# Two layers on one core: a merging step ahead of two modulation chunks, an output tile split by its last block, a pair product between two chunks

## The reference, cut to what matters

```
mod = silu(c) @ w_ada + b_ada                       # shifts, scales, gates
z, xbc, dt, sc_b, sc_c, sc_h, gate_a, gate_b = split(h @ w_in)
y   = gated_rmsnorm(ssd_chunked(silu(conv(xbc)), ...), z)      # 8 groups, 4 chunks of 128 tokens
y_a = y @ w_ssd_out
y_b = (sc_b * conv(sc_c * sc_h)) @ w_sc_out
merged = sigmoid(gate_a) * y_a + sigmoid(gate_b) * y_b
mix = merged @ w_o
x   = layer_norm(ALPHA * x + g1 * mix) * ln1_g + ln1_b
h   = layer_norm(x) * (1 + sc2) + sh2
scores = sigmoid(h @ router_w); top-k routing; 64 experts; shared expert
```

## Time and profile before

| | |
|---|---|
| median of 3 executions | 3117.07 us (3110.25 to 3120.41) |
| profiled execution, own time | 3117.96 us |
| its span | 3116.3 us |
| PE busy | 3010.0 us, 97% |
| DVE busy | 1901.8 us, 61% |
| mean granted clock of TensorE | 0.987 of full speed |

### The profile page before, as it was taken

The page is one execution under the profiler, slowest core; times in us unless marked ns, Lnnn a source line. Parts: engine busy times, 40 slices in busy tenths (PEclk is TensorE's granted clock), DMA queues, the critical chain, the costliest instruction groups (busy, mean ns, idle before and its releaser), DMA issues. The chain is left out here.

```text
span 3116.3 us, 41002 instructions
## 1 busy us (share of the span) xinstructions
PE 3010.0 (97%) x13039; PEld 1842.5 (59%) x13040; DVE 1901.8 (61%) x4044; ACT 583.8 (19%) x1348; POOL 245.6 (8%) x377
## 2 busy tenths in 40 slices
PE   7999999999999999999997998999999999999998
PEld 5767888755548333333332445488744788588543
DVE  5768888577657444334334377665657655665667
ACT  1002333211011122222221216310000233200000
POOL 1000000011100222222213000000000000000000
PEclk8999999999999999999999999999999999999999
DMA  7673232488733599999988321132254324022342
GB/s 258 181 217 124 67 108 87 137 288 288 254 147 146 209 382 382 378 384 370 395 342 285 115 87 56 34 102 81 108 188 156 102 80 142 30 101 81 149 175 108
DMA packets 260030, 570.90 MB, mean 183 GB/s; under 512 B 26969, under 2 KB 154564, under 8 KB 234170
## 3 DMA queue, kind: packets, MB, share of 16 engines
q1 hardware_dynamic: 202896, 415.82, 37.4%
q0 software_dynamic: 46992, 140.43, 12.9%
q10 hardware_dynamic: 10010, 12.92, 1.2%
HBM read 556.32 MB, written 38.93 MB: 191 GB/s over the span
## 5 line engine op out<-in xcount | busy, mean ns | idle before, releaser
L1709 PE MATMUL ps<-WR,hT 128*64 x832 | 373.5, 602 | 23.2 <-issue 21.7
L1710 PE MATMUL ps<-WR,hT 128*64 128x512 f32 x832 | 373.5, 602 | 0.0
L2154 PE MATMUL ps<-WR 128*128 128x512 f32 x784 | 337.4, 592 | 1.0 <-DVEq L3935 0.7
L1709 PEld LDWEIGHTS ps<-WR,hT 128*64 128x64 f32 x832 | 115.2, 139 | 265.0 <-issue 265.0
L2154 PEld LDWEIGHTS ps<-WR 128*128 128x128 f32 x784 | 148.6, 190 | 188.9 <-issue 186.1
L3647 DVE COPY WR<-WR 128x1024 f32 x208 | 130.9, 692 | 161.4 <-SPq L842 106.8
L2113 PE MATMUL ps<-WR 128*128 128x256 f32 x960 | 217.0, 379 | 0.0
L2113 PEld LDWEIGHTS ps<-WR 128*128 128x128 f32 x960 | 182.4, 190 | 24.8
L1730 PE MATMUL ps<-WR 128*64 x416 | 191.2, 603 | 2.8 <-DVEq L3660 1.8
L1731 PE MATMUL ps<-WR 128*64 128x512 f32 x416 | 191.3, 603 | 0.0
L3981 DVE TENSOR_TENSOR WR<-ps,WR 128x256 f32<-128x256 f32 x210 | 86.1, 423 | 145.0 <-PE ps L2113 143.2
(11 more groups left out here) (533 smaller groups left out, 5054.1 us busy)
## 6 DMA issues: line engine op xcount, KB each, us to landing
WR<-in_w_gate SPq DMA_DIRECT2D x64, 1024.0 KB, 8.5
WR<-in_w_up SPq DMA_DIRECT2D x64, 1024.0 KB, 10.9
WR<-in_w_down SPq DMA_DIRECT2D x64, 1024.0 KB, 10.2
WR<-in_mlp_w SPq DMA_DIRECT2D x56, 1024.0 KB, 6.8
WR<-in_mlp_w SPq DMA_DIRECT2D x20, 2048.0 KB, 8.2
xr<-in_ada_w POOLq DMA_DIRECT2D x32, 1024.0 KB, 5.6
WR<-in_w_in SPq DMA_DIRECT2D x24, 1024.0 KB, 7.5
WR<-in_w_in SPq DMA_DIRECT2D x40, 512.0 KB, 8.0
```

The lines of the kernel that those rows point to most:

```text
L1709: mm(out[0:HALF], xT[u][:, k, 0:HALF], wa[:, :, k, :], start=(k == 0), stop=(k == KD - 1))
L1710: last = mm(out[HALF:P], xT[u][:, k, HALF:P], wb[:, :, k, :], start=(k == 0), stop=(k == KD - 1))
L2154: return mm(ps[:, bank, :], rows, weights, start=(row == 0), stop=(row == PAST[phase] - 1))
```

## The change

It has three parts. First, in the last calls of turn 0 on PE the part 1 of the pair is cut in two: p7 goes between chunk 0 and chunk 1, and p3 and p4 stay behind chunk 1. In the other turns the order stays what it was. Second, the first output tile waits for seven merging steps instead of eight, takes the sum over partitions and blocks 0 to 6 of both halves, then waits for the eighth step and takes block 7 of both halves. Third, on DVE `merged(1)` goes ahead of the last two of six chunks of its step.

```diff
@@ ssd_pair on PE
-                else:
+                elif part == 1:
                     pe.wait_ge(*pair_sum(q, "s3"))
                     pe.wait_ge(*pair_c(q, "u2"))
                     product(r1, s3, t3, False)
+                else:
                     pe.wait_ge(*pair_sum(q, "s4"))
                     pe.wait_ge(*pair_c(q, "c5"))
                     product(r3, s4, hT_block(1, 1), False)
@@ ssd_turn on PE
                 if c == 0:
                     ssd_pair(p, 1, 0)
                     ssd_chunk(0, c)
+                    ssd_pair(p, 1, 1)
+                    ssd_chunk(1, c)
                 else:
                     ssd_pair(p, 0, 0)
                     ssd_pair(p, 0, 1)
+                    ssd_pair(p, 0, 2)
                     ssd_z_spent(c - 1)
                     ssd_chunk(0, c)
                     ssd_pair(p, 1, 0)
-                ssd_chunk(1, c)
-                ssd_pair(p, 1, 1)
+                    ssd_chunk(1, c)
+                    ssd_pair(p, 1, 1)
+                ssd_pair(p, 1, 2)
                 ssd_chunk(2, c)
@@ PE, after the merging
-            pe.wait_ge(sem("merge_free"), 2 + MERGES)
+            pe.wait_ge(sem("merge_free"), 2 + MERGES - 1)
             ada_sums(0, (MERGES - 1) * ADA_N + ADA_MERGE["sum"], SUM_BANKS[2])
             have("w_o", 0)
             have("w_o", 1)
-            out_tile("w_o", mergedT, 0, 0, 16)
+            for n in range(0, KD - 1):
+                out_tile("w_o", mergedT, 0, n, n + 1)
+            for n in range(KD, 2 * KD - 1):
+                out_tile("w_o", mergedT, 0, n, n + 1)
+            pe.wait_ge(sem("merge_free"), 2 + MERGES)
+            for n in (KD - 1, 2 * KD - 1):
+                out_tile("w_o", mergedT, 0, n, n + 1)
@@ DVE, merging
             gate_sums(0, 1)
-            weigh_part(1, 0, ADA_N)
+            weigh_part(1, 0, 4)
             merged(1)
+            weigh_part(1, 4, ADA_N)
```

## The result

The changed kernel takes 3123.01 us (median of 20 runs, 3113.24 to 3129.16), the kernel before 3116.5 us (20 runs, 3109.2 to 3124.62). The ratio is 1.0017, with a 95% interval of 1.0009 to 1.0025: slower by 3 to 8 us. I had forecast 3114.8 us, 2.3 us less, in a range up to 3121. By the bound of 0.3% this is still no change, but it moved the other way and lies outside the range.

What follows compares the result with a forecast made beforehand. PE, busy 97% of the span, was taken to bound the kernel through its order and waits. 0.5 + 2.8 + 0.2 - 1.2 = 2.3 us less, from 3117.07 to 3114.8 us; range 3108 to 3121.

Steps and rivals of the forecast that it cites:

- Part 1, 0.5 us: Turn 0: p7 covers PE's 1.06 us wait before chunk 1; z projection 0.5 us earlier, bounds 0 and 1.06.
- Part 2, 2.8 us (1.7 to 3.8): First merging iteration: merged(1) ahead of chunks 4 and 5 brings PE's second pair 2.8 us earlier, bounds 1.7 to 3.8.
- 1.0 us of stall: Merging: DVE's assumed wait for the load POOL issues after chunk 4, the middle of 0 to 2.1 us.
- The 4.2 us of PE: Merging: PE alone could reach the second pair at 688.3 instead of 692.43, by idle time and half clock removed.
- Part 3, direct gain 0.2 us: First output tile: ACT finds the first turned tile earlier while DVE waits for `grow`; 0.2 us gained, bounds 0 and 0.5.
- the 3.4 us that PE was to be early: First output tile: PE saves 1.75 us of idle time and 1.7 us of half clock, up to 3.4 us.
- Part 3, the clock, 1.2 us (0 to 2.1): Last `turn_in` and router: longer PE idle time brings half clock behind it, costing 1.2 us, bounds 0 to 2.1.
- I had 3.5: Ahead of the last `turn_in`: PE's idle time forecast at 3.5 us, from 4.2 less some spent earlier.
- The rival "slower": Router: clock stays at half throughout after longer idle time, adding 7.3 us, giving 3120.9 us; chance 0.05.
- `grow` moved with the merging: Rival at the first residual: `grow` lands no earlier, so the merging gain is lost; 3118.3 or 3117.1 us; chance 0.15.
- merged(1) never waited for PE: Rival in the merging: merged(1) comes before the PE product it needs, forecast as 2.8 us ahead; chance 0.02.

Runs made afterwards that it cites:

- e2: The kernel before with the split first output tile alone; 1.0021 (1.0012 to 1.0030) of the kernel before.
- e3: The kernel before with the second product pair of the shared expert's second tile moved behind the router, leaving PE idle; 1.0034 (1.0023 to 1.0044).
- e5: The kernel before with the moved merging step alone, merged(1) ahead of chunks 4 and 5; 1.0001 (0.9989 to 1.0012).
- e1: The changed kernel without the split first output tile; 0.9995 (0.9986 to 1.0005) of the kernel before.
- e6: The changed kernel without the split tile, with merged(1) behind chunk 4 instead of ahead of it; 0.9991 (0.9980 to 1.0002) of the kernel before.
- e9: The changed kernel without the split tile, DVE making corners and next sums after two chunks instead of three in the first merging iteration; 0.9993 (0.9981 to 1.0005).
- e11: e9 with two idle matmuls ahead of the last turned tile and four ahead of the routing counts; 0.9990 (0.9980 to 1.0001) of the kernel before.
- e10: The changed kernel with twelve idle matmuls, results unused, ahead of the last turned tile; 0.9995 (0.9984 to 1.0006) of the kernel before.
- e4: The changed kernel with a quarter of the shared expert's third tile brought ahead of the last turned tile; 1.0000 (0.9989 to 1.0012) of the kernel before.
- e7: The changed kernel with half of the shared expert's third tile brought ahead of the last turned tile; 1.0010 (0.9999 to 1.0022) of the kernel before.
- e8: The changed kernel again, nothing edited; 1.0013 (1.0003 to 1.0022) of the kernel before.
- e12: The changed kernel with e9's corner edit, twelve idle matmuls ahead of the last turned tile and four ahead of the counts; 0.9981 (0.9972 to 0.9991), 3110.62 us.

## Why the prediction was wrong

- **Part 1, 0.5 us.** Right: 0.42 us, with the wait for c21 as the next one, 0.72 us long. It is the same within 0.02 us in every trace with this part.
- **Part 2, 2.8 us (1.7 to 3.8).** Near in the profile after (3.1), but partly by luck. I bounded one load's lateness by a row on each side and took the middle, 1.0 us of stall, but looked only at the load behind chunk 4. It took 5.7 us and nothing waited for it. DVE waited 1.06 us all the same, for the loads ahead of it and behind it. The one behind chunk 5 was the late one, by up to 3.3 us in other traces, and I left out what can follow such a wait on PE: half clock again. The 4.2 us of PE also held 0.9 us and more of half clock behind p4's old wait, which isn't steady either: in e2 the same wait left the clock up. Over the seven traces that have the part as in the change, the pair comes 22.2 to 24.8 us behind the first sum, in the mean 23.7; in the three with the old order (before, e2, e3) 23.7 to 25.3, in the mean 24.8. That is 1.1 us. e5's 1.0001 (0.9989 to 1.0012) allows anything from no gain to the forecast one.
- **Part 3, direct gain 0.2 us.** Right, and for the reason given: DVE waits for `grow`. The last turned tile moved 3.76 us against the 3.58 of the first residual, 0.18 us more. Of the 3.4 us that PE was to be early, the 1.7 us of clock are no steady price of the old order: the wait of 1.74 or 1.75 us ahead of the unsplit tile was followed by half clock in three traces (before, e1, e6: 15.70 us) and not in four (e3, e5, e9, e11: 14.00 us).
- **Part 3, the clock, 1.2 us (0 to 2.1).** This is the step that failed. The chain was right, place for place: PE early, 3.1 us of idle time (I had 3.5) ahead of the last turned tile, the router at half clock. The size was wrong: 6.5 us. I bounded it by how long the lower clock had lasted after other gaps, and took the rows of wide products for it, where it was back after some 3 to 4 us. In the router, 64 records of 64 columns, it stayed down to the end and beyond, 17 us in all. The bound that no reason excluded was the whole router at half clock, 7.3 us. I had it as a rival at 0.05.
- **The sum.** The right mechanisms with 6.5 in place of 1.2 give 0.4 + 3.1 + 0.2 - 6.5 = 2.8 us more in the profiled execution, and 3.1 were read. With part 2 worth 1.1 us, the mean over the traces, it is 4.8 us, against 6.5 between the medians and 5.3 by the ratio (interval 2.8 to 7.8). The rival "slower" had 3120.9 us with part 2's gain still in it.
- **The other rivals.** `grow` moved with the merging, so nothing was lost there; merged(1) never waited for PE.

The page TensorE: Matmul & The Clock Gate of the Trainium skill (HAM oscillation) was the warning on this: it has waits of PE for a DMA bring the next work back to a cold start. e3 shows the same here by itself, behind a wait of 4.43 us for DVE. No run here tells what it would take in the router to bring the clock back, or why equal waits went either way.

## What to carry to other kernels

On a stretch where another engine sets the pace, making PE earlier only makes its idle time longer, and what that can cost is the work right behind the gap at half clock; if that work is on the path, count all of it. Before moving work to fill a gap, look whether it was filling another one; here twelve matmuls that nobody reads took the loss away (1.0017 to 0.9995), and moving useful work left it at 1.0000 and 1.0010. A wait removed ahead of a chain of loads should be priced with the slowest load of the chain, not the next one, and the order changed so that the consumer that others wait for stands ahead of it.

## What the runs showed of the hardware

- Ahead of the router, idle times of 0 to 1.58 us left the clock up in nine traces and idle times of 2.35 to 4.43 us took it down in five. Elsewhere it wasn't so even. The 1.74 or 1.75 us ahead of the first output tile took it down in three traces and left it up in four, 2.69 us ahead of e10's second pair left it up, and the 0.96 or 0.97 us ahead of the counts took it down in e6 and e10 and left it up in three others (before, e1, e5). The same wait of 2.15 us ahead of p4 left it up in e2 (first line) and took it down in e3 (second line):

```profile
675.93 1.99 PE L1391 MATMUL ps<-WR 128*128 128x256 f32 x8 [2.15 <-ACT WR L2508]
```

```profile
677.48 3.10 PE L1391 MATMUL ps<-WR 128*128 128x256 f32 x8 [2.15 <-ACT WR L2502]
```

- Once down, it came back in some 3 to 4 us in the wide products of the output tile and the pairs (in e4's second pair in some 6), in some 7 to 14 us over the routing counts and what follows them (e4, e6, e7, e10), and it stayed down for 17 us over router, transposes and the start of the shared products in four traces, for 20 in the fifth (e8).
- A load of 1 MB, issued at the same distance from the first sum, took 5.9 us in one execution (e12) and 8.7 in another (e7), and the load behind it was quick or slow with it.
